# One-piece modulation slabs, a rearranged attention section and aligned operands in a two-block transformer kernel

## What is computed

```python
def adaln(cvec, w, b, n):
    m = jax.nn.silu(cvec) @ w[:, : n * D_MODEL] + b[: n * D_MODEL]
    return jnp.split(m, n, axis=-1)
...
cmod = adaln(c_ctx, w_mod[l], b_mod[l], 2 if last else 6)
sh1, sc1, g1, sh2, sc2, g2 = [m[:, None, :] for m in adaln(c, w_mod[l], b_mod[l], 6)]
pa, q, k, v, pc = project(modulate(rms_norm_2(x_lat, norm1_g[l]), sh1, sc1), P, rope)
o = blocked_diff_attn(q, k_all, v_all, lam)
x_lat = x_lat + g1 * mixer_merge(pa, o, pc, P, lam_init)
x_lat = x_lat + g2 * conv_ffn(modulate(rms_norm_2(x_lat, norm2_g[l]), sh2, sc2), P)
```

## Time and profile before

| what | value |
|---|---|
| median of 3 runs (lowest, highest) | 2503.66 us (2502.77, 2505.79) |
| profiled execution | 2500.43 us, its span 2498.8 us |
| PE busy | 2247.9 us, 90% |
| DVE, ACT, POOL busy | 57%, 42%, 12% |
| mean granted clock of TensorE | 0.94 |
| DMA, moved | 349.15 MB, 44% of 16 engines |

### The profile page before, as it was taken

The page is one execution under the profiler, slowest core; times in us unless marked ns, Lnnn a source line. Parts: engine busy times, 40 slices in busy tenths (PEclk is TensorE's granted clock), DMA queues, the critical chain, the costliest instruction groups (busy, mean ns, idle before and its releaser), DMA issues. The chain is left out here.

```text
span 2498.8 us, 29164 instructions
## 1 busy us (share of the span) xinstructions
PE 2247.9 (90%) x11116; PEld 1796.6 (72%) x11116; DVE 1425.2 (57%) x2187; ACT 1044.5 (42%) x1664; POOL 303.8 (12%) x310
## 2 busy tenths in 40 slices
PE   8999898898999998979997877889989898887999
PEld 6777676787777776768876664667767787656997
DVE  5665574454465647545445886554444325966774
ACT  4545554443444455534443434322222223543443
POOL 0017120000000532210000540000000000600000
PEclk9999999999999999989998988889999998987999
DMA  7644335565555433466564213423333435333554
GB/s 227 185 124 127 105 115 160 181 177 183 191 175 157 141 102 95 138 201 180 160 205 159 63 51 93 135 93 110 101 101 110 135 101 168 94 119 117 162 183 161
DMA packets 184121, 349.15 MB, mean 140 GB/s; under 512 B 11824, under 2 KB 23216, under 8 KB 183984
## 3 DMA queue, kind: packets, MB, share of 16 engines
q1 hardware_dynamic: 183984, 347.29, 44.4%
HBM read 346.19 MB, written 1.05 MB: 139 GB/s over the span
## 5 line engine op out<-in xcount | busy, mean ns | idle before, releaser
L816 DVE TENSOR_TENSOR wlo<-wraw,whi 128x1024 fp32r<-128x1024 f32 (+1 forms) x538 | 646.2, 1207 | 682.0 <-ACT whi L1009 678.7
L1009 ACT ACTIVATE whi<-wraw 128x1024 fp32r<-128x1024 f32 (+1 forms) x552 | 562.7, 1027 | 648.0 <-PE psum L1770 546.3
L1770 PE MATMUL psum<-whi,act_h 128*128 128x512 f32 (+2 forms) x1424 | 578.4, 406 | 31.8 <-DVE p L1320 22.1
L1770 PE MATMUL psum<-wlo,act_h 128*128 128x512 f32 (+2 forms) x1424 | 564.7, 397 | 0.0
L1770 PE MATMUL psum<-whi,act_l 128*128 128x512 f32 (+2 forms) x1424 | 563.8, 396 | 0.0
L1770 PEld LDWEIGHTS psum<-whi,act_h 128*128 128x128 f32 x1424 | 277.1, 195 | 105.6 <-DVE p L1320 24.7
L1770 PEld LDWEIGHTS psum<-whi,act_l 128*128 128x128 f32 x1424 | 275.7, 194 | 62.2
L1770 PEld LDWEIGHTS psum<-wlo,act_h 128*128 128x128 f32 x1424 | 276.6, 194 | 56.5
L1770 PE MATMUL psum<-act_h,whi 128*128 128x512 f32 (+1 forms) x704 | 244.0, 347 | 23.7 <-DVE wlo L816 19.8
L1770 PE MATMUL psum<-act_l,whi 128*128 128x512 f32 (+1 forms) x704 | 242.2, 344 | 0.0
L1770 PE MATMUL psum<-act_h,wlo 128*128 128x512 f32 (+1 forms) x704 | 242.2, 344 | 0.0
(11 more groups left out here) (270 smaller groups left out, 2693.4 us busy)
## 6 DMA issues: line engine op xcount, KB each, us to landing
wraw<-in_w_in SPq DMA_DIRECT2D x136, 512.0 KB, 3.7
wraw<-in_w_gate SPq DMA_DIRECT2D x104, 512.0 KB, 3.7
wraw<-in_w_mod SPq DMA_DIRECT2D x96, 512.0 KB, 3.7
wraw<-in_w_ffn_in SPq DMA_DIRECT2D x80, 512.0 KB, 3.7
wraw<-in_w_ffn_out SPq DMA_DIRECT2D x44, 512.0 KB, 4.2
wraw<-in_w_down SPq DMA_DIRECT2D x44, 512.0 KB, 4.3
wraw<-in_w_val SPq DMA_DIRECT2D x40, 512.0 KB, 4.6
wraw<-in_w_branch SPq DMA_DIRECT2D x32, 512.0 KB, 3.9
```

What stands on the lines that cost most here:

```text
L816: eng.tensor_tensor(wlo[:, i, 0:st.n, 0:st.w], wraw[:, st.s % RING_W, 0:st.n, 0:st.w], whi[:, i, 0:st.n, 0:st.w].bitcast(F32), ALU.subtrac ...
L1009: nc.scalar.activation(whi[:, d % RING_S, 0:st.n, 0:st.w], wraw[:, s % RING_W, 0:st.n, 0:st.w], ACT.Copy).then_inc(sem("slab_rounded"), 1)
L1770: return nc.tensor.matmul(out, lhsT, rhs, start=start, stop=stop)
```

## The change

- Modulation is done in pieces of 128 columns by all 1024 rows. A piece is one slab of 512 KB, laid out contiguously on the host, and one product of 8 matmuls. `gemm` puts one piece after every fifth dense slab (after every second in the projections of the second block), preceded by the reader of the piece before it. Pieces and readers share one bank: bank 3 in the first block, bank 7 in the second. 64 pieces now ride in the first block, 8 in each projection stage and 8 in each feed-forward of the second block, 96 in all.
- The dense products of the first block rotate over three banks, (0, 1, 2). The second block has three free banks, (4, 5, 6), and its feed-forward rotates over seven.
- In the second block the four `ga` slabs, four of the eight tap parts, gelu, both layer norms, `agate`, `cback` and `csilu` stand between attention units, behind a unit's scores. Units all use the scores' banks (4, 5). Within a turn the order is transposes, scores, mix, values, where it was mix, transposes, scores, values.
- ACT copies all projected tiles to `p`.
- `cond` moves to the start of the first block.
- Padding: `at_offset` puts the tiles behind it at 384 modulo 512 bytes in a partition, and `rstd4` (16 bytes) moves from in front of `hid2_h` to behind `p`.

```diff
+OPERAND_AT, OPERAND_STEP = 384, 512
...
-        self.turns = (0, 1, 2, 3)
+        self.turns = (0, 1, 2)
+        self.free = FREE_BANKS
...
+            pl.mod_since += 1
+            if pl.mod_queue and pl.mod_since >= pl.mod_every:
+                pl.mod_since = 0
+                st.after = mod_ride(pl)
...
+def mod_ride(pl):
+    l, c = pl.mod_queue.pop(0)
+    steps = mod_reader(pl)
+    n = len(pl.mod_reads)
+    st = Step(kind="slab", s=len(pl.slabs), weight="w_mod_2", layer=l, c=c, evac="mod", mc=n, banks=[pl.bank(pl.mod_bank)],
+              first=True, last=True, war=pl.mod_reads[n - 2] if n >= 2 else [])
+    b, use = st.banks[0]
+    st.used = (f"psum_full{b}", use + 1)
+    pl.slabs.append(st)
+    pl.mod_last = st
+    return steps + [st]
...
+    pl.mod_queue = [(i, c) for i in range(DEPTH) for c in MOD_COLS]
...
+    pl.free, pl.mod_bank, pl.turns = (4, 5, 6), 7, (0, 1, 2, 3)
...
+        pl.mod_queue, pl.mod_every, pl.mod_since = [(l, c) for c in MOD_GATES[0]], 2, 0
         gc = project(C_C, T, ready)
         gq = project(C_Q, T)
         gk = project(C_K, 4)
-        ga = project(0, T)
         gv = project(C_V, 4)
...
+        ga = project(0, T)
...
+        beside = [ga[0], parts[4], ga[1], parts[5], ga[2], parts[6], ga[3], parts[7], gelu, aln[0], aln[1], agate, cback, cln[0],
+                  cln[1], Step(kind="csilu", l=l, tiles=T, n=cln[0].n)]
...
-            for kind, u in (("att2_m", i - 1), ("att2_t", i - 2), ("att2_s", i), ("att2_v", i - 2)):
+            for kind, u in (("att2_t", i - 2), ("att2_s", i), ("att2_m", i - 1), ("att2_v", i - 2)):
-                banks = {"att2_s": (4, 5) if u % 2 else (6, 7), "att2_m": (), "att2_t": (2,), "att2_v": (3,)}[kind]
+                banks = {"att2_s": (4, 5), "att2_m": (), "att2_t": (6,), "att2_v": (7,)}[kind]
...
+        pl.mod_queue, pl.mod_every, pl.mod_since = [(l, c) for c in MOD_GATES[1]], 5, 0
-        pl.turns = tuple(range(8))
+        pl.turns = tuple(range(7))
...
+            n = (OPERAND_AT - nc.sbuf_base) % OPERAND_STEP
+            if n:
+                sb(name, [P, n // 4], F32, stack)
...
-                        for t in range(0, st.tiles, 2):
+                        for t in range(st.tiles):
...
+                    fill(pe, bk)
+                    w = wraw[:, st.s % RING_W, :, :].rearrange("p k n -> p (k n)")
+                    for k in range(KD):
+                        r = 32 * (k % 4)
+                        ins = dot(psum[r:r + 32, bk[0], 0:P], condm[:, k, :], w[:, k * P:(k + 1) * P], k < 4, k >= 4)
+                    ins.then_inc(full(bk), 1)
```

More of the change, by code:

```diff
@@ L174, in gemm @@
             pl.slabs.append(st)
-            if evac != "mod":
-                st.d = len(pl.dense)
-                pl.dense.append(st)
+            st.d = len(pl.dense)
+            pl.dense.append(st)
             steps.append(st)
-    return steps
[L182 to L192, removed]
@@ new lines, in mod_reader @@
+def mod_reader(pl):
+    st, pl.mod_last = pl.mod_last, None
+    if st is None:
+        return []
+    l, c, part = st.layer, st.c, st.c // KD
+    bk = pl.bank(pl.mod_bank)
+    pl.mod_reads.append([(f"psum_full{bk[0]}", bk[1] + 1)])
+    if part in (2, 5):
+        return [Step(kind="mod_gate", l=l, c=c, mc=st.mc, gate=part // 3, j=c % KD, waits=drained(*st.banks), banks=[bk])]
+    steps = [Step(kind="mod_cols", l=l, c=c, mc=st.mc, waits=drained(*st.banks), banks=[bk])]
+    if part in (1, 4) and c % KD == KD - 1:
+        steps.append(Step(kind="mod_gain", l=l, i=part // 3, waits=drained(bk)))
@@ L509, in plan_second @@
         att += pending
[L511 to L519, removed]
-            late = g
-            if i == 1:
-                cback = Step(kind="cback", l=l, tiles=T, banks=[pl.gemm_bank() for i in range(T // 2)])
-                cln = ln(C_C, 2, drained(*cback.banks))
-                cout = Step(kind="csilu", l=l, tiles=T, n=cln[0].n)
-                stream += [cback, cln[0]]
-            if i == 2:
-                stream += [cln[1], cout]
-        stream += mod_reader(pl, late, pl.gemm_bank)
-        pl.steps += interleave(stream, att)
-        pl.turns = (0, 1, 2, 3)
-        mods = fill()
-        pl.steps += mods
+        assert not beside
+        pl.steps += att
         order = [0, 1, 6, 7, 2, 3, 4, 5]
@@ L591, in build @@
         plan_second(pl)
+    pl.steps = [one for st in pl.steps for one in [st] + st.after]
     slabs, dense = pl.slabs, pl.dense
@@ L750, in build @@
         gates2 = sb("gates2", [P, 2, 2, D], F32, two)
-        rstd4 = sb("rstd4", [P, 4], F32, two)
         with ExitStack() as own:
@@ L756, in build @@
         p = sb("p", [P, 4, IN_COLS], F32, two)
+        rstd4 = sb("rstd4", [P, 4], F32, two)
         kT = sb("kT", [P, B_HEADS, 4 * P], F32, two)
@@ L1779, in _ @@
                 if st.kind == "slab" and st.evac == "mod":
[L1781 removed]
+                    pe.wait_ge(sem("cond_silu"), 1)
                     pe.wait_ge(sem(f"slab_landed{st.s % RING_W}"), 16 * (st.s // RING_W + 1))
[L1783 to L1791 removed]
+                    bk = st.banks[0]
+                    fill(pe, bk)
[4 more added lines that the diff above has]
+                    ins.then_inc(full(bk), 1)
                 elif st.kind == "slab" and st.turned:
```

152 lines of the change are left out of this document (62 added, 90 removed).

## The result

| what | before | after |
|---|---|---|
| median (lowest, highest) | 2504.72 us (2502.77, 2508.26) | 2657.03 us (2655.67, 2658.33) |
| profiled execution, its span | 2500.43, 2498.8 us | 2655.67, 2654.0 us |
| mean granted clock | 0.94 | 0.93 |

The ratio is 1.061, 95% interval 1.0588 to 1.0625: the change makes the kernel 6% slower. The forecast was 2482, the range ended at 2532.

A forecast was written before the change was run, and what follows sets the result against it. PE was taken to bound the kernel (busy 90% of the span), with breaks at modulation chunks, second-block sections and product and norm boundaries. Terms -57.7 - 65 - 7 + 115 + 40 + 3 - 35 - 15 = -22 gave 2482 us, whole range 2425 to 2532.

The forecast's parts named there:

- Chunks in the feed-forward of layer 0: Second block: gaps at chunks (modulation work of four slabs at once) and half-clock work behind them go, -57.7 us.
- Chunks in the first block: Eight gaps at modulation chunks go in part, with some half-clock loss, -65 us.
- Norms of the second block: Two more norms lose their run of three `wlo`, 3.49 us each, -7 us.
- Pieces and readers: 96 pieces with readers at 1.2 us each, +115 us; DVE late at the reader, +40 (bounds 10 and 100).
- readers cost more: Rival, chance 0.13: each reader makes PE wait for DVE's queued work, 2525 us at the middle, 2557 at worst.
- The held slot: No term in the sum; three dense slabs, about 16.8 us, were taken to cover the next transfer, round and rest.
- Three banks: PE waits where DVE or ACT clear a product's first tile late in the first block's attention, +3 us.
- Distance of two matmuls: Padding to 384 modulo 512 bytes shortens 6144 matmuls of 512 columns from 0.233 to 0.227 us, -35 us.
- the padding would have done nothing: Rival, chance 0.06: the offset is not the cause, or the skill page's rule holds, 2517 us.
- Projection and attention of the second block: Rearranged projection and attention, -7 us in layer 0 and -8 in layer 1, -15 in all.
- one score pair costs: Rival, chance 0.09: PE can't give DVE the next scores before the exponentials are out, 48 us more, 2525.
- More gain: Rival, chance 0.27: DVE and ACT catch up in PE's pauses at readers, and sections overlap better, 2432 us.

The follow-up runs named there:

- e3: The kernel before with only the padding (operand tiles at 384 modulo 512 bytes): 2477.35 us, 0.9876.
- e10: The kernel of e9, with ga slabs, taps and norms placed behind a unit's mix in place of behind its scores: 2427.81 us, 0.9678.
- e7: The kernel of e3, with the first block's products over three banks in place of four: 2481.22 us, 0.9890.
- e2: The changed kernel with five raw weight slots in place of four, still shared by pieces and dense slabs: 2578.09 us, 1.0271.
- e5: The changed kernel, but SP fetches a piece three dense slabs later, and rounding and rest count dense slabs alone: 2588.71 us, 1.0329.
- e9: The changed kernel with e5's later fetch and readers two dense slabs behind their piece (one in projections), keeping the change's projection and attention: 2465.18 us, 0.9819.
- e11: The kernel of e8, with all attention units on the score banks (4, 5): 2436.19 us, 0.9715.
- e8: The changed kernel with e5's later fetch, later readers as in e9, and the kernel before's projection and attention code: 2432.40 us, 0.9703.

## Why the prediction was wrong

By its own terms, against the median before:

- **Chunks in the feed-forward of layer 0, -57.7: right.** Its 1056 matmuls at 0.227 us are 239.7 us. The stage takes 297.9 in e3, so the chunks cost 58, and 252.2 in e10, so a piece with its reader costs 1.6 there.
- **Chunks in the first block, -65: right, as far as it can be told.** The first block with its last norm ends at 1338.7 in e10 and 1342.8 in e7 (three banks and padding, with chunks). 64 pieces of about 0.57 + 0.28 us are 54, so the chunks cost about 58.
- **Norms of the second block, -7: right.** The stretches that hold the two norms fell from 64.7 and 140.5 us in e3 to 61.7 and 135.9 in the change, together 7.6.
- **Pieces and readers, +115 and +40: too small by about 56.** The parts priced at 0.57 and 0.28 were right for the first block. The gate readers were not looked at by themselves: 0.60 for 0.28 us, 32 times, is 10. And the waits were 119 us for my 33 + 40. In the first block the median of reader to piece was 0.68 us, close to my 0.62, in the second 1.28. At the median idle times, 0.41 and 0.68 us, the 63 and 28 waits would be 45 us for my 33, and the other 74, for my 40, are lateness. So what was mis-sized is above all lateness. I had listed the places where DVE is behind by itself, and took behind a plain slab none. A part of it comes from late transfers, over ACT's round and DVE's `wlo`: with five slots (e2) the waits are 101 us. For the rest the timelines show taps and copies ahead of the reader in DVE's order (1505.80 to 1516.73), which no run took away by itself. The rival (readers cost more, 2525, deciding from 0.23 us a piece) named this mechanism and had 0.13. It came true at 46 / 96, or about 0.5 us a piece.
- **The held slot: the step that failed, +68 (e5; 79 by e2) where the sum had nothing.** The prediction said that a piece leaves three dense slabs of 24 matmuls, 16.8 us, while the next transfer, rounding and rest run. That is so with four token tiles, and I carried it over, without its sum, to the 76 of the 96 pieces that stand behind slabs of two tiles. With two tiles a slab is 12 matmuls of 0.227 us, or 24 of 0.12, about 2.8, and three are 8.3 us, against 94.03 to 100.95 us, that is 6.9, from the request to the rest. And the cover doesn't protect what stands in ACT's order behind the rounding. I had read the mechanism in the earlier trace rows, as the cost of a chunk, and had not asked what a piece does to the same slots. Of the 4-tile stages, the feed-forward of layer 0 took 267.2 us in the change, 267.7 in e5: there the hold cost nothing, as I had said. In the projection and attention of that layer, where pieces come every second slab, it cost 8 (261.8 and 253.7).
- **Three banks, +3: small, as forecast, but not sized.** 4 us by the medians of e3 and e7, 10 by their first blocks, against a bound of 12.
- **Distance of two matmuls, -35: right in cause, a quarter too large in size** (26, e3). The distance is 0.227 at all operands, as forecast, also where `whi` is stationary. In the first block, with 3984 of the 6144 matmuls, only 12 us came (1329.1 to 1317.5) and not the 23 of my sum, though the distance there is 0.227: 116 us of it ran at half clock in e3 and 104 before. By the rule of the Trainium skill (page "TensorE: Matmul & The Clock Gate", section "Wait — 56ns, not 53.3ns?"), 215.7 ns at 512 columns, the padding would have done nothing. The section opens from bf16 matmuls, and for the fp32r matmuls here the runs disagree: 26 us by moving tiles, and still no product at 215.7 (every median distance at 512 columns is 227 in e3).
- **Projection and attention of the second block, -15: wrong, +25.** The step that failed is the count of a turn. I added up the durations in a turn, and took the longest engine as its length. The trace's turn is a chain over PE, ACT and DVE, and I didn't ask in which place of DVE's order the taps stand. They stood ahead of the mix, and PE waited 74 us. e9 against e10 shows 37 us for that alone. The rival (one score pair costs, 2525) was wrong in its mechanism: e11 found nothing.

The sizes add up: 56 for the readers, 68 for the hold, 40 for attention and 9 for the distance are 173, and the forecast missed by 175. This is closer than the terms are known: hold and readers share waits (e2), and the 7 us that the chunks of the first block and the 7 that three banks may have cost beyond their prices are not in it.

The range failed with the sum. It took each unknown near its price and let them cancel, but readers, hold and attention all erred to the same side. All three need DVE, ACT or SP to be in time in one common order. That they have one cause is not shown: by e8 the losses add. "More gain" with 0.27 rested on DVE being busy for only 57%, which says nothing on a lump ahead of a reader.

## What to carry to other kernels

A step put into a fixed common order must be followed on every engine and queue: what it holds from its request to its use, and what stands behind it in each order. Here the same work took 229 us more or less by three choices that change no instruction's cost: fetched when needed, read back some slabs later, and the side work laid behind the operation that the next PE step waits for. A cover counted in slabs has to be worked out again for each width and number of tiles in which the slab occurs.

## What was not expected of the hardware

The place of the fp32r operand tiles is worth 0.233 against 0.227 us for a matmul of 512 columns, whether they stand still or move, and 26 us of the kernel (e3). At 256 columns it went the other way: the last feed-forward of the second block took 127.9 us before and 129.4 in e3, and the median distance in it went from 0.117 to 0.120 us. Why either happens is open.
